# Expert-choice ranks computed two projections early, their sums on ScalarE and their one-hots on GpSimd

## What is computed

```python
def expert_choice_ffn(h, w_router, w_gate, w_up, w_down):
    cap = CAPACITY_FACTOR * S // N_EXPERTS            # 128 of 1024 tokens
    logits = jnp.einsum('bsd,de->bse', h, w_router, preferred_element_type=jnp.float32)
    aff = jax.nn.softmax(logits, axis=-1)
    gate, tok = lax.top_k(jnp.swapaxes(aff, 1, 2), cap)
    xin = h[bidx, tok]
    a = jnp.einsum('becd,edf->becf', xin, w_gate)     # 2048 -> 1024
    u = jnp.einsum('becd,edf->becf', xin, w_up)
    y = jnp.einsum('becf,efd->becd', jax.nn.silu(a) * u, w_down)
    y = y * gate[..., None].astype(y.dtype)
    return jnp.zeros_like(h).at[bidx, tok].add(y)
```

## Time and profile before

| | us |
|---|---|
| median of 3 runs | 2770.07 (2770.07 to 2770.69) |
| the profiled execution | 2770.87 |
| its span, first to last instruction | 2768.8 |
| mixer and output projection, up to the first product of expert 0 | 1566 |
| expert stage up to the last product | 1168 |
| tail: last tiles normalised and stored | 35 |

### The profile page before, as it was taken

The page is one execution under the profiler, slowest core; times in us unless marked ns, Lnnn a source line. Parts: engine busy times, 40 slices in busy tenths (PEclk is TensorE's granted clock), DMA queues, the critical chain, the costliest instruction groups (busy, mean ns, idle before and its releaser), DMA issues.

```text
span 2768.8 us, 33660 instructions
## 1 busy us (share of the span) xinstructions
PE 2684.0 (97%) x12353; PEld 2213.9 (80%) x12353; DVE 2093.9 (76%) x2787; ACT 1423.5 (51%) x1605; POOL 485.6 (18%) x746
## 2 busy tenths in 40 slices
PE   9999999999999999999999889999999999999996
PEld 7888888888888888788888777787777777777784
DVE  7775676587777667834375779888899889889987
ACT  6433221122322367733233466776777677777776
POOL 1432112211111446501010100111111001011001
PEclk9999999999999999999999999999999999999998
DMA  9688776898887785245353699999999999999998
GB/s 366 240 297 296 257 265 226 286 340 281 290 302 262 250 263 180 94 150 182 134 174 135 267 379 375 367 376 368 380 393 387 376 378 383 372 377 382 388 390 352
DMA packets 251123, 827.75 MB, mean 299 GB/s; under 512 B 30342, under 2 KB 55445, under 8 KB 227933
## 3 DMA queue, kind: packets, MB, share of 16 engines
q1 hardware_dynamic: 210528, 685.12, 66.3%
q0 software_dynamic: 40432, 140.49, 15.1%
HBM read 728.16 MB, written 99.91 MB: 299 GB/s over the span
## 4 chain that ended last, share of the span: by engine, by line
PE 79%; DVE 12%; ACT 3%; issue 2%; DMA 2%; POOL 1%; SPq 0%; ACTq 0%; DVEq 0%; POOLq 0%
PE ps L3210 14%; DVE elo L2674 8%; PE ps L2847 6%; PE ps L2846 6%; PE ps L2848 5%; PE ps L2842 5%; PE ps L2843 5%; PE ps L2844 5%; PE ps L3062 4%; PE ps L3064 4%; PE ps L3063 4%; PE ps L3241 4%; PE ps L3239 4%; PE ps L3240 4%; PE ps L2897 2%
## 5 line engine op out<-in xcount | busy, mean ns | idle before, releaser
L2674 DVE TENSOR_TENSOR elo<-eraw,ehi 128x2048 fp32r<-128x2048 f32 x384 | 873.6, 2290 | 123.6 <-ACT ehi L1785 114.8
L1785 ACT ACTIVATE ehi<-eraw 128x2048 fp32r<-128x2048 f32 x384 | 733.1, 1919 | 318.7 <-PE ps L3210 235.8
L1413 ACT ACTIVATE whi<-raw 128x1024 fp32r<-128x1024 f32 x159 | 168.6, 1060 | 577.8 <-PE ps L2848 246.2
L3210 PE MATMUL ps<-ehi,xh 128*128 128x512 f32 x960 | 384.0, 400 | 0.0
L3210 PE MATMUL ps<-elo,xh 128*128 128x512 f32 x960 | 381.5, 397 | 0.0
L1894 DVE TENSOR_TENSOR wlo<-raw,whi 128x1024 fp32r<-128x1024 f32 x159 | 194.6, 1224 | 185.1 <-ACT whi L1413 184.4
L3210 PE MATMUL ps<-ehi,xl 128*128 128x512 f32 x960 | 260.7, 394 | 0.0
L3210 PEld LDWEIGHTS ps<-ehi,xh 128*128 128x128 f32 x960 | 185.7, 193 | 38.8
L3210 PEld LDWEIGHTS ps<-elo,xh 128*128 128x128 f32 x960 | 185.5, 193 | 38.8
L3210 PEld LDWEIGHTS ps<-ehi,xl 128*128 128x128 f32 x960 | 183.3, 191 | 39.0
L3062 PE MATMUL ps<-ohi,a_hi 128*128 128x512 f32 x512 | 202.9, 396 | 0.9 <-DVE olo L2396 0.9
(11 more groups left out here) (496 smaller groups left out, 5503.0 us busy)
## 6 DMA issues: line engine op xcount, KB each, us to landing
raw<-in_w_stream SPq DMA_DIRECT2D x271, 512.0 KB, 5.0
eraw<-in_w_gate SPq DMA_DIRECT2D x256, 512.0 KB, 6.9
eraw<-in_w_up SPq DMA_DIRECT2D x256, 512.0 KB, 8.6
eraw<-in_w_down SPq DMA_DIRECT2D x128, 1024.0 KB, 7.7
oraw<-in_w_stream SPq DMA_DIRECT2D x128, 256.0 KB, 2.6
xt<-in_xT SPq DMA_DIRECT2D x48, 256.0 KB, 4.4
scr_ops<-xt POOLq DMA_DIRECT2D x48, 256.0 KB, 3.1
nav<-scr_rows SPq DMA_DIRECT2D x128, 64.0 KB, 4.0
```

What stands on the lines that cost most here:

```text
L1413: act.activation(whi[:, c % SPL, :], raw_pair(c)[0], ACT.Copy).then_inc(S["w_hi"], 1)
L1785: act.activation(ehi[:, p % ERING, :], flat2(eraw[:, 2 * (p % EDEEP):2 * (p % EDEEP) + 2, :]), ACT.Copy)\
L2674: dve.tensor_tensor(elo[:, p % ERING, :], flat2(eraw[:, 2 * (p % EDEEP):2 * (p % EDEEP) + 2, :]), ehi[:, p % ERING, :].bitcast(F32), ALU.s ...
L3210: last = pe.matmul(gu_bank(e, c), a[:, k, :], w[:, p % ERING, c * BW:(c + 1) * BW], start=(k == 0 and a is hi and w is ehi), stop=(k == KD ...
```

## The change

The ranks of experts 2 to 15 are made two gu blocks before their products instead of one, in smaller pieces and by three engines:

- `compare_later(e, n, part)` on DVE does the compares of expert e + 2 during gu of expert e, one instruction after each pair from k = 1 to 12, into a wide 16-bit tile `above` (512 columns of greater-than, 128 of the tie rule), without a sum.
- `rank_sum(e, n)` on ACT copies `above` onto itself with a sum into `ranks`, after k = 5, 8, 11 and 14 (`SUMAT`).
- POOL's own `place_ranks` makes the four one-hots, behind the gather of the expert before. `fetch_row` is issued for the expert after the next.
- Experts 0 and 1 keep the old form (`compare`, DVE's `place_ranks`), both ahead of expert 0's products; PE transposes a second row of chances (`turn_row(1)`) for it, and PE's first gu pair waits for the marks of expert 1.
- `list_products(e + 1)` moves from after k = 7 to after k = 6 (for e = 0 from 6 to 1), `merge(e + 1)` from k = 8 to 7 (from 7 to 2), the overlap test of the last two experts by two pairs later.
- `list_in` and `place_hot` are bfloat16: the chance in three parts and the token in two, five columns in place of four. POOL splits the chances (`split_gates`), which DVE did in part. `merge` sums two groups of columns, one instruction and one wait more.

```diff
+SUMAT = (5, 8, 11, 14)
+            def split_gates():
+                pool.wait_ge(S["gate_high"], BEFORE["gate_high"] + 1)
+                pool.tensor_tensor(gate_rest[:, :, :], chosen[:, :, :], list_in[:, :, 0, :], ALU.subtract).then_inc(S["pool_step"], 1)
...
             def fetch_row(e):
                 pool.wait_ge(S["row_saved"], BEFORE["row_saved"] + 16)
-                pool.wait_ge(S["marked"], BEFORE["marked"] + MARKS * e)
                 pool.dma_start(chances[:, :], t["chance_rows"][e, :].partition_broadcast(P)).then_inc(S["row_in"], 16)
+            def place_ranks(e):
+                pool.wait_ge(S["summed"], BEFORE["summed"] + 4 * (e - 1))
+                pool.wait_ge(S["listed"], BEFORE["listed"] + e)
+                for n in range(4):
+                    pool.tensor_scalar(out=place_hot[:, n, :], in0=countdown[:, :], scalar1=ranks[:, n:n + 1], scalar2=None,
+                                       op0=ALU.is_equal).then_inc(S["ranked"], 1)
             gather(0)
+            fetch_row(2)
             for e in range(1, NE):
-                fetch_row(e)
+                if e + 1 < NE and e > 1:
+                    pool.wait_ge(S["compared"], BEFORE["compared"] + MARKS * (e - 1))
+                    fetch_row(e + 1)
                 pool.wait_ge(S["xtr"], BEFORE["xtr"] + 4 * e)
                 if e >= 3:
                     add_outputs(e - 3)
                 gather(e)
+                if e + 1 < NE:
+                    place_ranks(e + 1)
...
+            def rank_sum(e, n):
+                if n == 0:
+                    act.wait_ge(S["ranked"], BEFORE["ranked"] + 4 * e)
+                act.wait_ge(S["compared"], BEFORE["compared"] + MARKS * (e - 2) + 3 * n + 2)
+                act.activation(above[:, n % 2, :], above[:, n % 2, :], ACT.Copy, accum_out=ranks[:, n:n + 1]).then_inc(S["summed"], 1)
...
+                if kind == "gu" and e + 2 < NE and k in SUMAT:
+                    rank_sum(e + 2, SUMAT.index(k))
...
+            def compare_later(e, n, part):
+                own, upto, turn, to = chosen[:, n, e:e + 1], n * P, 4 * (e - 2) + n, above[:, n % 2, :]
+                if part == 0:
+                    if n == 0:
+                        dve.wait_ge(S["row_in"], BEFORE["row_in"] + 16 * (e - 1))
+                    if turn >= 2:
+                        dve.wait_ge(S["summed"], BEFORE["summed"] + turn - 1)
+                    dve.tensor_scalar(out=to[:, upto:BW], in0=chances[:, upto:BW], scalar1=own, scalar2=None, op0=ALU.is_gt)\
+                        .then_inc(S["compared"], 1)
...
+            for n in range(4):
+                compare(1, n)
+            place_ranks(1)
...
-                if kind == "gu" and e + 1 < NE:
-                    at = k if e == 0 else k - 1
-                    if 0 <= at < 4:
-                        compare(e + 1, at)
-                    elif at == 4:
-                        place_ranks(e + 1)
-                    elif at == 7:
-                        merge(e + 1)
+                if kind == "gu" and e + 1 < NE and k == (2 if e == 0 else 7):
+                    merge(e + 1)
+                if kind == "gu" and e + 2 < NE and 1 <= k < 13:
+                    compare_later(e + 2, (k - 1) // 3, (k - 1) % 3)
...
-                    if e + 1 < NE and k == (6 if e == 0 else 7):
+                    if e + 1 < NE and k == (1 if e == 0 else 6):
                         list_products(e + 1)
```

More of the change, by code:

```diff
@@ L11 @@
 F32R = mybir.dt.float32r
+BF16 = mybir.dt.bfloat16
 U32 = mybir.dt.uint32
@@ L2628, in place_ranks @@
                                       op0=ALU.is_equal).then_inc(S["ranked"], 1)
+            def compare_later(e, n, part):
[7 more added lines that the diff above has]
+                        .then_inc(S["compared"], 1)
+                elif part == 1 and n:
+                    dve.tensor_scalar(out=to[:, 0:upto], in0=chances[:, 0:upto], scalar1=own, scalar2=None, op0=ALU.is_ge)\
+                        .then_inc(S["compared"], 1)
+                elif part == 2:
+                    dve.scalar_tensor_tensor(out=to[:, BW:BW + P], in0=chances[:, upto:upto + P], scalar=own, in1=lower[:, :],
+                                             op0=ALU.is_equal, op1=ALU.mult).then_inc(S["compared"], 1)
             def merge(e):
                 from_last, own = list_bank(e), slice(e, e + 1)
-                gate, ahead, apart = (merged[:, j:j + 1] for j in range(3))
+                gate, ahead, apart, token = (merged[:, j:j + 1] for j in range(4))
                 dve.wait_ge(S["listed"], BEFORE["listed"] + e + 1)
-                dve.tensor_reduce(out=gate, in_=from_last[:, 0:2], axis=AX.X, op=ALU.add).then_inc(S["dve_step"], 1)
-                dve.tensor_tensor(apart, first_token[:, own], from_last[:, 2:3], ALU.subtract).then_inc(S["dve_step"], 1)
+                dve.tensor_reduce(out=gate, in_=from_last[:, 0:3], axis=AX.X, op=ALU.add).then_inc(S["dve_step"], 1)
+                dve.tensor_reduce(out=token, in_=from_last[:, 3:5], axis=AX.X, op=ALU.add).then_inc(S["dve_step"], 1)
                 step.settle()
                 step.settle()
+                dve.tensor_tensor(apart, first_token[:, own], token, ALU.subtract).then_inc(S["dve_step"], 1)
                 dve.tensor_tensor(ahead, first_gate[:, own], gate, ALU.is_ge).then_inc(S["dve_step"], 1)
@@ L2642, in merge @@
                 step.settle()
-                dve.scalar_tensor_tensor(out=tokf[:, own], in0=apart, scalar=ahead, in1=from_last[:, 2:3], op0=ALU.mult, op1=ALU.add)\
+                step.settle()
+                dve.scalar_tensor_tensor(out=tokf[:, own], in0=apart, scalar=ahead, in1=token, op0=ALU.mult, op1=ALU.add)\
                     .then_inc(S["dve_step"], 1)
@@ L3165, in list_products @@
                     pe.wait_ge(S["ranked"], BEFORE["ranked"] + 4 * e + n + 1)
[L3166 removed]
+                    last = pe.matmul(list_bank(e)[:, 0:5], place_hot[:, n, :], list_in[:, n, 0:5, e], start=(n == 0), stop=(n == 3))
                 last.then_inc(S["listed"], 1)
```

78 lines of the change are left out of this document (45 added, 33 removed).

## The result

| | before | after |
|---|---|---|
| median, us | 2770.38 (2770.07 to 2770.99) | 2697.91 (2696.18 to 2699.9) |
| profiled execution | 2770.87 | 2698.79 |
| its span | 2768.8 | 2697.1 |
| first product of expert 0 | 1566.0 | 1568.1 |
| from there to the last product | 1167.8 | 1090.4 |

The ratio is 0.9738, with a 95% interval of 0.9722 to 0.9755.

A forecast was written before the change was run, and what follows sets the result against it. The prediction took PE, with DVE and transfers near full, to bound the expert stage, PE stalling at the lists. 59.6 + 6.9 - 3 = 63.5 us off 2770.07 gave 2706.6 us, range 2699 to 2725.

The forecast's parts named there:

- What bounds the kernel: Expert stage: PE, DVE and transfers all near full; PE stalls 38.2 us in 15 pieces at list products, awaiting DVE's one-hots.
- The rival that splits would set the pace: Expert stage: compares, sums and exclusion delay ACT and DVE, PE waits, clock falls; 42 of 63.5 us lost, 2749; chance 0.08.
- Part 1: List products in the expert stage: all 15 waits and the clock drops behind them go; gain 59.6 us, bounds 54 and 63.
- Part 2: Expert 1's transposes: its list and gather come five pairs earlier, so PE's wait for the tokens goes; gain 6.9 us.
- Parts 3 and 4: Expert stage: DVE's spread compares and ACT's sums fit into idle time and keep PE's pace; 0 us on the path.
- Part 5: Expert stage: POOL's one-hots take 1.6 us an expert, hidden, without delaying DVE; by the exclusion rule 11 and 1.6 us.
- Part 6: Expert stage and tail: transfers have 56 us in reserve, fall about 10 us behind PE, and the tail loses 3 us.
- Rival (a): Expert stage: transfers become the bound, with a reserve of 35 us and not 56; 2724 us; chance 0.17.
- (c): List products: one-hots come early but products still wait, for the output bank or fetched row; 2768 us; chance 0.03.
- (d): Expert stage: PE is granted a lower clock without a stop; slower, 2822 us at a mean of 0.90; chance 0.03.
- The sum: Whole kernel: 59.6 + 6.9 - 3 = 63.5 us gained, giving a median of 2706.6 us; chance 0.69.

The follow-up runs named there:

- The three stops: Three kernels: the changed kernel with a wait ahead of the list products, stops of 1.72, 1.92 and 4.70 us; 2743.44, 2741.51 and 2784.86 us.
- the long stop: The changed kernel with PE waiting ahead of the list products for DVE's compare of k = 6, stops of 4.70 us; 2784.86 us.
- the run with less work for PE: The changed kernel without the third pass (low part of the activations) of pair k = 10 in each gu block; 2696.83 us.

## Why the prediction was right or wrong, point by point

**What bounds the kernel: right, in part.** PE's stops at the lists were the path, and they went without a successor among the engines. The rival that splits would set the pace fell with them: the stage has no wait of PE for elo after the change, and with DVE's lump of compares untouched, in the kernel that only shifts the list, a single one of 0.14 us.

**Part 1, the list stalls: the mechanism right, the size wrong, and this is the step that failed.** The term was 59.6; the trace shows 70.4. 6.0 us of the 10.8 lie in the second pair behind a stop. I wrote "The rest is the four products and a pair at a low clock", took the loss from the distance to the next last pass, and let the windows behind the 15 products only decide which kind each was. Six of the ten cases show 3.41 to 3.98 us there in place of 2.72; the one whose rows I had read, is one of those without. The three stops confirm the reading: the slow stretch wanders between the first pair and the second with a constant sum. 0.9 us is that the ten cases of the first kind lose 5.08 in the mean up to the next last pass, not the 4.98 of the one I showed (the expectation of the long stop has 5.15, which is too much). The other 3.9 us are the products, 0.24 a list and not 0.5. There the comparison with transposes was good for 32-bit products (0.50 in the shifted kernel) and didn't hold for the new type; even the lower bound of 0.25 was the measured value. A bound of the loss itself was missing altogether: 54 to 63 held only the products' doubt, and so 2699 was too near.

**Part 2, expert 1's tokens: right in its place, and less in the end.** 6.9 was expected, 7.25 came in the stage; undone, it costs 4.6, since 3.2 us of the tail's loss go with it.

**Parts 3 and 4, DVE and ACT: right.** 0.48 us and 0.90 for what was put at 0.48 and 0.95, and 0 on the path. The eleven compares of an expert take 3.9 us together, not 3.1, and stay under the 5.2. The two elements per cycle that part 3 cites from the Trainium skill (VectorE: DVE Perf Modes, What auto-detection actually checks) come with a 16-bit result too: 281 ns for 128 columns and 481 for 512 are 0.52 ns a column, as in the plain rows.

**Part 5, POOL: right on the path, wrong in itself.** For each expert I had 1.6 us of POOL and nothing of DVE; 4.2 and 0.24 were measured. The estimate by the Trainium skill's rule, 11 and 1.6, took every one-hot to wait for a split and to hold one up; the rule holds, but only 17 of the 56 one-hots waited, and 14 splits. The row of 395 ns was short by itself: alone this one-hot takes 591.

**Part 6, the transfers: the number right within 1 us, by luck.** The tail lost 3.6 where 3 was said, but not as I worked it out. I expected late loads of x tiles to delay the squares; these run as before, and it is the stores that land late behind them. The reserve of 56 us was too small: PE gave up 77 and the median landing times of the weights rose by 7.4, so about 70 was there, an estimate. Both kernels' windows hold the same 33 MB in the second queue, whose share came to 12.5% of 1054 us = 132 before and 11.7% of 980 = 115 after. A share is not a fixed cost.

**Rival (a): not what happened, and nearer than I said.** No weight was late. But the run with less work for PE shows where this rival begins, 3 to 4 us of stage before the point that the change reaches: what PE gains from there on comes back in the tail. **(c) and (d) fell:** no wait moved, and the clock is 1.00 from 1652 to 2590 us.

**The sum.** 63.5 + 10.8 (part 1) + 0.35 (part 2) - 0.6 (tail) = 74.1; the profiled executions differ by 72.1 with the 2.1 us of scatter ahead of the stage, the medians by 72.5. With the 10.8 of part 1 in it the forecast would have been 2695.8, 2.1 us from what was measured.

**What each part of the change is worth.** 58.8 of some 74 us come from the later place of products and merge, four numbers in the old kernel. The earlier list of expert 1 gives 4.6. These two are differences of medians; the next three are read from timelines: the ranks of expert 1 ahead of the stage, which end the stop at its list, some 6; a merge that is in time for the test of the last two experts, 1.1 against the kernel that only shifts the list; 16-bit lists 14 x 0.27 = 3.8. The one-hots on POOL give nothing. That the spread compares and ACT's sums are worth anything is not shown: with the old lump a gu block takes 41.31 us against 41.03 to 41.05, and the products explain the difference.

## What to carry to other kernels

Price a stop of TensorE by the sum over everything until its pace is back, not by the next distance: here a stop of 1.7 to 4.7 us cost about 2 us more, in most cases, in a slow stretch that fell into one pair or two. Where a consumer waits for a short side product, first ask whether it can be consumed two steps later; that was four fifths of the gain, without moving any work. And when stops are removed, add up stage and tail: once the sum stays while the stage shrinks, transfers are the bound, and the next gain lies where their engines are idle.

## What the hardware showed that I had not expected

- In the profiled executions a stop of 1.72 us brought the granted clock down 13 times of 13, one of 1.92 us 11 of 12, one of 4.7 us 12 of 12, and one of 2.53 us, before the change, 8 of 13. One of 2.34 us, seen once, did not, nor did one of 0.9 us.
- A 16-bit list of four products interrupts the 512-column stream for 0.24 us, a 32-bit one for 0.50; each further product costs 0.027.
- GpSimd's one-hots and VectorE's splits exclude each other: 591 ns alone, 1987 to 2745 in the 17 cases of 56 that waited for a split, and 14 splits up to 0.29 us longer.
- The sixteen DMA engines held 405 GB/s with 11.7% of small and indirect transfers among them, and 426 to 429 in windows of 4 us.
